# Two of four chunk inversions moved among the blocks of two projections

## The chip, the cores and the metric

One core of a Trainium2 chip runs the kernel. The metric is the device time of one execution in microseconds, as the median of several runs.

## What is computed

Two transformer blocks over 512 tokens of width 1024. The change lies in the first, whose mixer has two halves:

```python
proj = rms_norm(x, norm_w) @ w_in          # dn_q, dn_k, dn_v, dn_z, beta, decay, sw_q, sw_k, sw_v, sw_z
q, k, v = split(silu(conv5(dn_q, dn_k, dn_v)))   # depthwise over time
q = l2_norm(q) * 128 ** -0.5; k = l2_norm(k)     # 4 heads of 128
# gated delta rule, forwards and backwards (2 directions), by chunks
t_inv = inverse(I + strict_tril(beta * k k^T * decay))
a_intra = tril(q k^T * decay)
state, o = scan over the chunks with t_inv, a_intra, k, v
dn = rms_norm(fwd + bwd) * silu(dn_z)
# banded attention: window 128, 8 query heads, 2 key heads of 64, with sinks
sw = softmax_with_sink(rope(rms(sw_q)) @ rope(rms(sw_k))^T, band) @ sw_v * silu(sw_z)
x = x + concat(dn, sw) @ w_out
```

The kernel takes chunks of 128 tokens, so there are four (cb 0 to 3), each in two directions d.

## The kernel before

All engines walk one list, `ORDER`, that Python code builds by calling `do(name, ...)`. Each engine has its own function for a step's name and emits its part, so the order of the list is the order of every engine's queue: TensorE, ACT, DVE and POOL (GpSimd) are in-order, and SP issues the loads. Semaphores (`Mark`) carry the dependences. PSUM has eight banks of 128x512; `Ring.take` hands them out in turn, and the first writer of a bank waits until its last reader is done (`emptied`).

Matmuls of the projections are in three parts: every weight unit is loaded to RAW, rounded to WH by ACT (`prep`), and WL = RAW - WH is made by POOL; there are four slots. `w_ahead(u)` puts the preparation of unit u in the list, two units ahead of its use. Products of activations are taken as hi*hi + hi*lo + lo*hi.

Stages around the change, in order of the list:

- Units 8 to 19, `ch`: twelve groups of 128 channels of dn_q, dn_k, dn_v. `conv` of group j-1 stands behind `ch` of group j: ACT copies the bank with the centre tap, DVE adds four taps (line 1332), ACT applies silu, `square` (ACT) follows for groups 0 to 7. Between them stand `gates` (two steps, softplus, sigmoid and cumulated decays) and `swa_prep` (13 steps: four `rope_sq`, one root, then a scale and a turn for each of four token blocks: DVE on SWR, R1, R2).
- `tok` of SZ (units 20 to 23) and Z (24 to 27): four weight units by four token blocks in banks 0 to 3. I call the 6 matmuls of one unit and one token block a block. Each group of 16 ends with ACT's silu of the four banks into MIX.
- `qk_norm` beside SZ: `qsum` (TensorE sums squares over channels, ACT takes the logarithm), then `qexp` (ACT Exp, then the product into QK on POOL for even j and DVE for odd j). `to_tok` turns v and k to tokens, `rope_t` the attention's q and k; ACT copies each bank out. They stand in `g1`, beside Z.
- `invert(cb)`: 19 steps. Two `inv_decay` (TensorE broadcasts the decays, ACT Abs and Exp give EE, POOL makes MB with two operations), `inv_kq` (k k^T and q k^T), `inv_m` (DVE MP, POOL adds the identity, DVE masks DD, ACT rounds MR), `inv_mt` (turned MP), six doubling levels, each `inv_x` (8 matmuls, two DVE masks) and `inv_d` (16 matmuls, three ACT copies and one of DVE), `inv_x7`, `inv_t`. The work buffers of chunks 1 and 2 lie in the weight slots WH and WL, so they wait for the last block of Z.
- `swa`: 32 pieces (4 query blocks by 8 heads) as `swa_s` (scores in bank 5, maximum on DVE, Exp on ACT), `swa_t`, `swa_o`; a block of 8 heads is closed by DVE, and POOL multiplies it into MIX. 96 steps.
- Before, the four inversions take turns, one step each with two of `swa` behind it. Then `z_gain` (four POOL products) and the scan (`scan_keys`, `scan_v`, `scan_o`), which starts with POOL's `vb`.

Of the kernel before, what the change touches and what calls it, by code (L numbers as in the profile page):

```python
# [199 lines left out]
def program(nc, x, wflat, cfd, ppd, prd, wsd, tbd, seld, out):  # L200
# [9 lines left out]
    C0 = 48  # L210
# [45 lines left out]
    KT = zb("kt", [128, 4, 512], F32, 72)  # L256
    VT = zb("vt", [128, 4, 512], F32, 80)
    SL8 = [zb(f"sl{j}", [128, 512], F32, 72 + 2 * j) for j in range(8)]
# [5 lines left out]
    SKT = zb("skt", [128, 512], F32, 127)  # L264
# [21 lines left out]
    MP = [zb(f"mp{c}", [128, 2, 512], F32, 4 * c) for c in range(4)]  # L286
    AT = [zb(f"at{c}", [128, 2, 512], F32, 16 + 4 * c) for c in range(4)]

    def work(i, *at):
# [9 lines left out]
            work(3, two_at(zb, 104), two_at(zb, 108), two_at(sb, C0 + 16.25), (zb, (112, 124)))]  # L299
# [4 lines left out]
    OT = zb("ot", [128, 512], F32, 129)  # L304
# [242 lines left out]
    for j in range(12):  # L547
        w_ahead(U_CH + j + 2)
        G.take(("ch", U_CH + j), (conv_v, (j, 4)))
        do("ch", U_CH + j, "n0", 1)  # L550
        if j:
            do("conv", j - 1)
            if 2 <= j <= 9:
                do("square", j - 2)
        if j in (1, 3):
            step(g2)
        if j:
            step(g3, 2 if j > 6 else 1)
# [4 lines left out]
    G.over((0, 1, 2, 3))  # L563
    g1 = in_turn(qk_norm(), to_tokens("v"), rope_turn(), to_tokens("k"))

    def tok_part(u0, n, by, *sides):
        ids, i = G.ids, G.i
        G.over((0, 1, 2, 3))
        for tb in range(4):
            G.take(("tok", u0, tb), by(tb))  # L570
        G.ids, G.i = ids, i
        for k in range(4):
            w_ahead(u0 + k + 2)
            do("tok", u0, k, "n0", SLOT0, n)
            for g, m in sides:
                step(g, m)

    G.over((4, 5, 6, 7))
    tok_part(U_SZ, 512, lambda tb: (proj, ("sz", tb)), (g1, 3))
    gi = [invert(cb) for cb in (0, 3, 1, 2)]  # L580
    BI.over((4,))
    ids, i = G.ids, G.i
    G.over((0, 1, 2, 3))
    for tb in range(4):
        G.take(("tok", U_Z, tb), (proj, ("z", tb)))
    G.ids, G.i = ids, i
    for k in range(4):
        w_ahead(U_Z + k + 2)
        do("tok", U_Z, k, "n0", SLOT0, 512)
        step(g1, 4)  # L590
        if k in (1, 2):
            step(gi[0])
    while step(g1):
        pass
    step(gi[1], 2)
    BI.over((0, 1, 2, 3, 4))
    gs = swa()
    for b in (5, 6, 7):
        BANK[("swa", b)] = (b, emptied[b])
    for g in gi[2:]:  # L600
        step(g, 2)
    live = True
    while live:
        live = False
        for g in gi:
            live = step(g) or live
            step(gs, 2)
# [328 lines left out]
    def pool_engine(e):  # L936
# [25 lines left out]
        def inv_decay(cb, d):  # L962
            W = WORK[cb]
            ee, mb = W["EE"][d][:], W["MB"][d][:]
            on.wait_ge(*inv_a.at(("ee", cb, d)))
# [30 lines left out]
        def scan_keys(d, r):  # L996
            cb = chunk(d, r)
            W = SCAN[d]
            if r == 0:
                on.wait_ge(*inv_v.at(("t", 0, 1)))  # L1000
                on.wait_ge(*inv_v.at(("t", 2, 1)))
                on.wait_ge(*swa_g.at(3))
            else:
                on.wait_ge(*scan_p.at(("av", d, r - 1)))
            on.wait_ge(*gate_v.at("beg"))
            on.wait_ge(*gate_a.at("egl"))
            on.wait_ge(*tok_a.at(("k", cb)))
            on.wait_ge(*tok_a.at(("v", cb)))
            k3 = h3(KT[:, cb, :])
            if r:  # L1010
                e.tensor_tensor(h3(W["KB_"][:]), k3, b4r(BEG[:, d, cb, :]), ALU.mult).then_inc(scan_g.up(("kb", d, r)), 1)
            e.tensor_tensor(h3(W["VB"][:]), h3(VT[:, cb, :]), b4r(BETA[:, d, cb, :]), ALU.mult).then_inc(scan_g.up(("vb", d, r)), 1)
            if r < 3:
                e.tensor_tensor(h3(W["KD"][:]), k3, b4r(EGL[:, d, cb, :]), ALU.mult).then_inc(scan_g.up(("kd", d, r)), 1)
# [25 lines left out]
    def scalar_engine(e):  # L1040
# [67 lines left out]
        def to_tok(what, cb):  # L1108
            b, _ = BANK[(what, cb)]
            on.wait_ge(*tok_p.at((what, cb)))  # L1110
            on.wait_ge(*qk_g.at(6))
            on.wait_ge(*qk_v.at(7))
            act((VT if what == "v" else KT)[:, cb, :], psum[b][:, :], ACT.Copy, tok_a.up((what, cb)))
# [32 lines left out]
        def tok(u0, i, which, ks, n):  # L1146
            if i < 3 or u0 in (U_OUT, U_OUT2):
                return
# [15 lines left out]
        def inv_decay(cb, d):  # L1164
# [3 lines left out]
            on.wait_ge(*gate_v.at("ngc"))  # L1168
            if cb in (1, 2):
# [22 lines left out]
        def swa_s(n):  # L1192
# [3 lines left out]
            if n > 1:  # L1196
                on.wait_ge(*swa_p.at(("t", n - 2)))
            act(PM[n % 2][:, 0:nk], psum[5][:, 0:nk], ACT.Exp, swa_a.up(("p", n)), bias=MX[:, qb, h:h + 1], scale=0.125,
# [104 lines left out]
        def finish(tb):  # L1303
            for n in range(2):
# [10 lines left out]
                    gate1=gate1, gate2=gate2, rope_root=rope_root, rope_t=rope_t, tok=tok, inv_decay=inv_decay, inv_m=inv_m,  # L1315
# [6 lines left out]
    def vector_engine(e):  # L1322
# [849 lines left out]
```

## Time and profile before

| | us |
|---|---|
| median of 3 runs | 1100.96 |
| lowest and highest | 1096.2, 1101.19 |
| the profiled execution | 1095.42 |
| its span, first to last instruction | 1093.6 |
| TensorE busy | 1014.5 (93%) |
| DVE, ACT, POOL busy | 459.4, 448.7, 414.0 |
| mean granted clock of TensorE | 0.976 |

The rows below are of the profiled execution. Its span starts with the first instruction; 1.8 us lie around it. PE is TensorE's matmuls, PEld its weight loads; PEclk is the granted clock as a share of 2.4 GHz. A row of the timeline has the start, the busy time, the engine, the line of the kernel, the operation, its output and inputs, their shapes and how many instructions are merged; in brackets the idle time ahead of it and who ended it. Matmul rows overlap each other by pipelining. Lines 1044, 1326, 1329, 1332 and 1722 belong to helpers that emit ACT activations, DVE operations and matmuls, so rows are told apart by tile names.

### The profile page before, as it was taken

To read this page: it belongs to the slowest core of one execution; us is meant where nothing else is said; L and a number is where in the kernel's file an instruction comes from. 1 tells how busy PE (TensorE), PEld (TensorE's weight loads), DVE (VectorE), ACT (ScalarE), POOL (GpSimd) and SP (SyncE) were. 2 spreads that over 40 slices of the span, in tenths; PEclk is the share of its full clock that TensorE was granted. 3 is DMA by queue.
4 is the path that set the end of the run, shared out by engine and by line. 5 is a ranking of instruction groups with operands and counts; after the bars stand their busy time and mean duration, and the time that the engine had idled before them with its cause. 6 is when DMAs were issued, how large, how long until landed. Compare 5 with 4: busy or idle time off the path is not lost.

```text
span 1093.6 us, 12916 instructions
## 1 busy us (share of the span) xinstructions
PE 1014.5 (93%) x5326; PEld 839.0 (77%) x5326; DVE 459.4 (42%) x744; ACT 448.7 (41%) x800; POOL 414.0 (38%) x221
## 2 busy tenths in 40 slices
PE   5999779759999899979999999989999999999997
PEld 4887557647889898868777767878888888888876
DVE  5046922077666536240112263243333333474434
ACT  5356337724445226244234443244343434342223
POOL 2565325543002144353432323244443435354440
PEclk9999989869999999999999999989999999999999
DMA  7422212000000005332221101123323232322212
GB/s 258 149 61 83 69 58 78 1 0 1 1 1 1 1 1 183 119 115 76 78 77 59 58 1 58 58 96 99 115 79 114 81 112 83 110 96 96 96 38 77
DMA packets 22730, 80.41 MB, mean 74 GB/s; under 512 B 2480, under 2 KB 2736, under 8 KB 22544
## 3 DMA queue, kind: packets, MB, share of 16 engines
q1 hardware_dynamic: 21808, 77.95, 21.9%
q10 hardware_dynamic: 864, 1.64, 0.4%
q8 instruction: 42, 0.69, 0.3%
q14 instruction: 16, 0.13, 0.0%
HBM read 77.48 MB, written 2.10 MB: 73 GB/s over the span
## 4 chain that ended last, share of the span: by engine, by line
PE 78%; DVE 12%; ACT 7%; POOL 1%; issue 1%; DMA 1%; DVEq 0%; ACTq 0%
PE bank L1722 75%; PE bank L1730 3%; DVE qk L1332 2%; DVE swr L1326 1%; ACT L1044 1%; DVE vc L1332 1%; DVE xl L1326 1%; DVE dd L1326 1%; DVE xs L1332 1%; ACT ee L1044 1%; ACT qk L1044 1%; ACT xs L1044 1%; ACT wh L1044 1%; DVE mp L1326 1%; DVE r L1326 1%
## 5 line engine op out<-in xcount | busy, mean ns | idle before, releaser
L942 POOL TENSOR_TENSOR wl<-raw,wh 128x1024 fp32r<-128x1024 f32 (+1 forms) x131 | 315.3, 2412 | 472.2 <-ACT wh L1044 472.1
L1722 PE MATMUL bank<-xh,wh 128*128 128x512 f32 (+1 forms) x536 | 207.2, 387 | 8.7 <-DVE xl L1326 4.8
L1722 PE MATMUL bank<-xl,wh 128*128 128x512 f32 (+1 forms) x536 | 206.4, 385 | 0.0
L1722 PE MATMUL bank<-xh,wl 128*128 128x512 f32 (+1 forms) x536 | 206.3, 385 | 0.0
L1044 ACT ACTIVATE wh<-raw 128x1024 fp32r<-128x1024 f32 (+1 forms) x131 | 135.4, 1043 | 140.1 <-PE bank L1722 140.0
L1722 PE MATMUL bank<-wh,xh 128*128 128x512 f32 (+1 forms) x352 | 139.5, 396 | 16.6 <-DVE xl L1326 7.2
L1722 PE MATMUL bank<-wh,xl 128*128 128x512 f32 (+1 forms) x352 | 135.8, 386 | 0.0
L1722 PE MATMUL bank<-wl,xh 128*128 128x512 f32 (+1 forms) x352 | 135.7, 385 | 0.0
L1722 PEld LDWEIGHTS bank<-xh,wh 128*128 128x128 f32 x536 | 102.0, 190 | 30.3 <-issue 7.5
L1722 PEld LDWEIGHTS bank<-xh,wl 128*128 128x128 f32 x536 | 102.0, 190 | 19.7
L1722 PEld LDWEIGHTS bank<-xl,wh 128*128 128x128 f32 x536 | 102.0, 190 | 19.4
L1722 PEld LDWEIGHTS bank<-wh,xh 128*128 128x128 f32 x352 | 67.8, 193 | 32.2 <-issue 11.7
L1722 PEld LDWEIGHTS bank<-wh,xl 128*128 128x128 f32 x352 | 67.5, 192 | 13.1
L1722 PEld LDWEIGHTS bank<-wl,xh 128*128 128x128 f32 x352 | 67.5, 192 | 12.8 <-issue 0.9
L1326 DVE TENSOR_TENSOR al<-ac,ah 128x512 fp32r<-128x512 f32 x22 | 53.6, 2447 | 51.8 <-ACT ah L1044 51.8
L1722 PE MATMUL bank<-wh,ah 128*128 128x512 f32 x176 | 68.5, 389 | 2.9 <-DVE al L1326 2.9
L1722 PE MATMUL bank<-wl,ah 128*128 128x512 f32 x176 | 68.5, 389 | 0.0
L1722 PE MATMUL bank<-wh,al 128*128 128x512 f32 x176 | 68.5, 389 | 0.0
L1332 DVE SCALAR_TENSOR_TENSOR ta<-bank,pparams,ta 128x510 f32<-128x510 f32 (+1 forms) x44 | 32.9, 749 | 72.5 <-ACT ta L1044 71.8
L1332 DVE SCALAR_TENSOR_TENSOR tgg<-bank,pparams,tgg 128x510 f32<-128x510 f32 (+1 forms) x44 | 33.0, 749 | 62.4 <-ACT tgg L1044 61.6
L1044 ACT ACTIVATE tgg<-bank,pparams 128x512 f32<-128x512 f32 x22 | 17.2, 781 | 78.8 <-PE bank L1722 78.8
L1628 DVE TENSOR_REDUCE mx<-bank 128x1 f32<-128x128 f32 (+3 forms) x32 | 15.7, 491 | 74.9 <-PE bank L1722 74.9
(224 smaller groups left out, 1507.6 us busy)
## 6 DMA issues: line engine op xcount, KB each, us to landing
raw<-in_wflat SPq DMA_DIRECT2D x127, 512.0 KB, 3.5
h<-in_x SPq DMA_DIRECT2D x4, 512.0 KB, 5.4
h<-in_x SPq DMA_DIRECT2D x1, 2048.0 KB, 8.7
gain<-in_pr SPq DMA_DIRECT2D x3, 512.0 KB, 3.7
consts<-in_cf SPq DMA_DIRECT2D x1, 1472.0 KB, 7.0
raw<-in_wflat SPq DMA_DIRECT2D x4, 272.0 KB, 3.3
out<-outt ACTq DMA_DIRECT2D x4, 256.0 KB, 2.1
out<-outt SPq DMA_DIRECT2D x4, 256.0 KB, 2.1
```

The costliest lines, as they stand in the source:

```text
L942: e.tensor_tensor(WL[u % NS][:, 0:n], RAW[u % NS][:, 0:n], WH[u % NS][:, 0:n].bitcast(F32), ALU.subtract).then_inc(w_lo.up(u), 1)
L1044: return e.activation(out_, in_, f, **k).then_inc(up, 1)
L1326: return e.tensor_tensor(out_, a, b, op).then_inc(up, 1)
L1332: return e.scalar_tensor_tensor(out_, a, s, b, op0, op1).then_inc(up, 1)
L1628: e.tensor_reduce(mx, psum[FA_BANKS[n % 2]][:, 0:(qb + 1) * 128], AX.X, ALU.max, negate=True).then_inc(fa_v.up(("m0", n)), 1)
L1722: return e.matmul(o, l, r_, start=start, stop=stop, skip_group_check=part)
L1730: return e.transpose(o, in_, cf("ident")[0:in_.shape[0], 0:in_.shape[0]])
```

## The change

The chunks are taken in another place. `swa_prep` gives one step for each channel group from the first on, and the two `gates` steps move from groups 1 and 3 to groups 6 and 8. SZ and Z are emitted block by block: six blocks carry `qk_norm` (and two mask steps of chunk 3), the other 26 carry chunks 0 and 3, alternately one and two steps per block. Banks 4 to 7 serve `qsum` and these inversions. After the last block come the masks of chunks 1 and 2, the turning of v, rope and k (13 copies), and then chunks 1 and 2 take turns with three `swa` steps behind each.

The buffers of the stage are laid out anew: the squares SL8 lie where chunk 0's work buffers are (ACT's masks of chunk 0 wait for the last use of SL8), K and V by tokens lie in XH and XL (their copies wait for the last block of Z), chunk 3's work lies on R1, R2 and on attention's PM and PMT (POOL's mask waits for the last turn, the first two Exp of attention for chunk 3's end), and MP and AT of chunks 0 and 3 lie where KT and VT were.

```diff
-    KT = zb("kt", [128, 4, 512], F32, 72)
-    VT = zb("vt", [128, 4, 512], F32, 80)
-    SL8 = [zb(f"sl{j}", [128, 512], F32, 72 + 2 * j) for j in range(8)]
+    KT = [zb(f"kt{c}", [128, 512], F32, (12, 14, 16, 18)[c]) for c in range(4)]
+    VT = [zb(f"vt{c}", [128, 512], F32, (28, 30, 0, 2)[c]) for c in range(4)]
+    SL8 = [zb(f"sl{j}", [128, 512], F32, 32 + 2 * j) for j in range(8)]
...
-    MP = [zb(f"mp{c}", [128, 2, 512], F32, 4 * c) for c in range(4)]
-    AT = [zb(f"at{c}", [128, 2, 512], F32, 16 + 4 * c) for c in range(4)]
+    MP = [zb(f"mp{c}", [128, 2, 512], F32, (72, 4, 8, 76)[c]) for c in range(4)]
+    AT = [zb(f"at{c}", [128, 2, 512], F32, (80, 20, 24, 84)[c]) for c in range(4)]
...
-            work(3, two_at(zb, 104), two_at(zb, 108), two_at(sb, C0 + 16.25), (zb, (112, 124)))]
+            work(3, two_at(zb, 116), two_at(zb, 120), two_at(sb, C0 + 16.25), two_at(zb, 124))]
...
-        if j in (1, 3):
+        step(g3)
+        if j in (6, 8):
             step(g2)
-        if j:
-            step(g3, 2 if j > 6 else 1)
     do("conv", 11)
     for g in (g2, g3):
         while step(g):
             pass
-    G.over((0, 1, 2, 3))
-    g1 = in_turn(qk_norm(), to_tokens("v"), rope_turn(), to_tokens("k"))
...
-    G.over((4, 5, 6, 7))
-    tok_part(U_SZ, 512, lambda tb: (proj, ("sz", tb)), (g1, 3))
-    gi = [invert(cb) for cb in (0, 3, 1, 2)]
-    BI.over((4,))
...
-        do("tok", U_Z, k, "n0", SLOT0, 512)
-        step(g1, 4)
-        if k in (1, 2):
-            step(gi[0])
+    G.over((4, 5, 6, 7))
+    BI.over((4, 5, 6, 7))
+    gi = [invert(cb) for cb in (0, 3, 1, 2)]
+    g1 = qk_norm()
+
+    def both(*gs):
+        live = True
+        while live:
+            live = False
+            for g in gs:
+                if step(g):
+                    live = True
+                    yield
+
+    def tok_parts(u0, name):
...
+        for k in range(4):
+            w_ahead(u0 + k + 2)
+            for tb in range(4):
+                do("tok_b", u0, k, "n0", SLOT0, 512, tb)
+                yield
+        do("evac", u0)
+
+    dense_parts = in_turn(tok_parts(U_SZ, "sz"), tok_parts(U_Z, "z"))
+    for n in range(6):
+        step(dense_parts)
+        step(g1, 2)
+        if n in (2, 4):
+            step(gi[1])
     while step(g1):
         pass
-    step(gi[1], 2)
+    g03 = both(gi[0], gi[1])
+    n = 0
+    while step(dense_parts):
+        n += 1
+        step(g03, 2 if n % 2 else 1)
+    gs = swa()
+    g1 = in_turn(to_tokens("v"), rope_turn(), to_tokens("k"))
     BI.over((0, 1, 2, 3, 4))
-    gs = swa()
+    G.over((0, 1, 2, 3, 4))
+    step(gi[2], 2)
+    step(g1, 2)
+    step(gi[3], 2)
+    step(g1, 2)
...
+    while step(g1):
+        pass
...
-    for g in gi[2:]:
-        step(g, 2)
     live = True
     while live:
         live = False
-        for g in gi:
+        for g in gi[2:]:
             live = step(g) or live
-            step(gs, 2)
+            step(gs, 3)
     do("z_gain")
...
             on.wait_ge(*tok_p.at((what, cb)))
-            on.wait_ge(*qk_g.at(6))
-            on.wait_ge(*qk_v.at(7))
-            act((VT if what == "v" else KT)[:, cb, :], psum[b][:, :], ACT.Copy, tok_a.up((what, cb)))
+            on.wait_ge(*dense.at((U_Z + 3, 3)))
+            act((VT if what == "v" else KT)[cb][:], psum[b][:, :], ACT.Copy, tok_a.up((what, cb)))
...
             on.wait_ge(*gate_v.at("ngc"))
+            if cb == 0:
+                on.wait_ge(*qk_g.at(6))
+                on.wait_ge(*qk_v.at(7))
             if cb in (1, 2):
                 on.wait_ge(*dense.at((U_Z + 3, 3)))
...
             if n > 1:
                 on.wait_ge(*swa_p.at(("t", n - 2)))
+            else:
+                on.wait_ge(*inv_v.at(("t", 3, 1)))
...
             on.wait_ge(*inv_p.at(("q", cb)))
-            on.wait_ge(*dense.at((U_Z + 3, 3)))
+            if cb in (1, 2):
+                on.wait_ge(*dense.at((U_Z + 3, 3)))
```

## Rows read from the trace of the kernel before

**Rows 1.** The page: shares of the chain of waits by engine.

```profile
PE 78%; DVE 12%; ACT 7%; POOL 1%; issue 1%; DMA 1%; DVEq 0%; ACTq 0%
```

**Rows 2.** Busy time by stretch: stretch, length, PE, PEld, DVE, ACT, POOL, clock, DMA.

```profile
145.65:200.75 55.10, 54.24 (x241) 41.49 (x242) 5.95 (x5) 36.16 (x57) 25.46 (x14) 0.95 0.18 58
200.75:250.60 49.85, 30.27 (x179) 24.18 (x177) 28.27 (x48) 22.29 (x59) 29.45 (x25) 0.76 0.00 0
250.60:372.97 122.37, 121.62 (x972) 107.58 (x973) 79.60 (x160) 57.98 (x139) 15.00 (x12) 1.00 0.00 1
```

**Rows 3.** Timeline of DVE beside the channel groups.

```profile
62.68 3.10 DVE L1332 SCALAR_TENSOR_TENSOR qk<-bank,pparams,qk 128x510 f32<-128x510 f32 x4 [36.09 <-ACT qk L1044]
...
72.75 3.10 DVE L1332 SCALAR_TENSOR_TENSOR qk<-bank,pparams,qk 128x510 f32<-128x510 f32 x4 [0.24 <-ACT qk L1044]
...
78.60 3.10 DVE L1332 SCALAR_TENSOR_TENSOR qk<-bank,pparams,qk 128x510 f32<-128x510 f32 x4 [1.91 <-ACT qk L1044]
...
102.58 0.81 DVE L1326 TENSOR_TENSOR swr<-swr,ssq 128x640 f32<-128x640 f32 x1
...
110.89 3.02 DVE L1326 TENSOR_TENSOR swr<-swr,ssq 128x640 f32<-128x640 f32 x1
...
119.31 2.96 DVE L1326 TENSOR_TENSOR swr<-swr,ssq 128x640 f32<-128x640 f32 x1
...
135.21 3.05 DVE L1326 TENSOR_TENSOR swr<-r,r 128x128 f32<-128x128 f32 x2
```

**Rows 4.** Timeline of TensorE: three column sums (two instructions each), twice.

```profile
145.71 5.38 PE L1722 MATMUL bank<-sl,consts 128*128 128x512 f32 x6 [1.45 <-DVE vc L1332]
...
156.40 2.74 PE L1722 MATMUL bank<-sl,consts 128*128 128x512 f32 x6
```

**Rows 5.** Timeline of ACT: tables, logarithms, Exp, and one mask.

```profile
147.28 1.28 ACT L1044 ACT_TABLE_LOAD   x1
148.58 0.69 ACT L1044 ACTIVATE sl<-bank,ceps 128x512 f32<-128x512 f32 x1
...
176.58 2.18 ACT L1044 ACTIVATE sl<-sl 128x512 f32<-128x512 f32 x4
...
187.96 1.17 ACT L1044 ACTIVATE ee<-bank,ngc 128x128 f32<-128x128 f32 x4
189.16 0.63 ACT L1044 ACTIVATE ee<-ee 128x512 f32<-128x512 f32 x1
```

**Rows 6.** Timeline of POOL: weight subtraction, products of Q and K, mask.

```profile
152.84 2.40 POOL L942 TENSOR_TENSOR wl<-raw,wh 128x1024 fp32r<-128x1024 f32 x1 [3.15 <-ACT wh L1044]
...
176.14 4.69 POOL L947 TENSOR_TENSOR qk<-qk,sl 128x512 f32<-128x512 f32 x3 [2.90 <-ACT sl L1044]
...
189.87 1.28 POOL L966 TENSOR_TENSOR mb<-ee,consts 128x512 f32<-128x512 f32 x1 [2.92 <-ACT ee L1044]
191.23 1.04 POOL L968 TENSOR_TENSOR mb<-mb,nbeta 128x512 f32<-128x512 f32 x1
```

**Rows 7.** Timeline of DVE and POOL: the preparation of one chunk.

```profile
231.97 1.28 DVE L1326 TENSOR_TENSOR mp<-bank,mb 128x512 f32<-128x512 f32 x2
234.03 2.34 DVE L1326 TENSOR_TENSOR dd<-mp,consts 128x512 fp32r<-128x512 f32 x2 [0.78 <-POOL mp L980]
...
232.73 2.49 POOL L980 TENSOR_TENSOR mp<-mp,consts 128x512 f32<-128x512 f32 x2 [2.41 <-DVE mp L1326]
```

**Rows 8.** TensorE: four blocks (chain of waits); two scores, four x steps (timeline).

```profile
180.10 5.46 PE bank L1722 x24
...
336.50 0.70 PE L1722 MATMUL bank<-skt,sqt 64*128 64x256 f32 x2
...
339.72 0.70 PE L1722 MATMUL bank<-skt,sqt 64*128 64x256 f32 x2
...
351.17 3.74 PE L1722 MATMUL bank<-dt,mr 128*128 128x128 f32 x32
```

**Rows 9.** Timeline of POOL: the four gains and the scan's first product.

```profile
346.96 5.02 POOL L987 TENSOR_TENSOR mix<-mix,rparams 128x512 f32<-128x512 f32 x4
378.59 1.04 POOL L1012 TENSOR_TENSOR vb<-vt,beta 128x512 f32<-128x512 f32 x1 [26.61 <-DVE mp L1326]
```

More of the change, by code:

```diff
@@ L263, in program @@
     R2 = zb("r2", [128, 640], F32, 124.5)
-    SKT = zb("skt", [128, 512], F32, 127)
+    SKT = zb("skt", [128, 512], F32, 128)
     SQT = zb("sqt", [128, 4, 512], F32, 64)
@@ L303, in program @@
     SWO = zb("swo", [128, 512], F32, 122)
-    OT = zb("ot", [128, 512], F32, 129)
+    OT = zb("ot", [128, 512], F32, 116)
     SCAN = [dict(VB=zb("vb0", [128, 512], F32, 32), KB_=zb("kb0", [128, 512], F32, 34), KD=zb("kd0", [128, 512], F32, 36),
@@ L562, in program @@
             pass
-    G.over((0, 1, 2, 3))
-    g1 = in_turn(qk_norm(), to_tokens("v"), rope_turn(), to_tokens("k"))
-    def tok_part(u0, n, by, *sides):
+    G.over((4, 5, 6, 7))
[11 more added lines that the diff above has]
+    def tok_parts(u0, name):
         ids, i = G.ids, G.i
@@ L569, in tok_part @@
         for tb in range(4):
-            G.take(("tok", u0, tb), by(tb))
+            G.take(("tok", u0, tb), (proj, (name, tb)))
         G.ids, G.i = ids, i
@@ L573, in tok_part @@
             w_ahead(u0 + k + 2)
-            do("tok", u0, k, "n0", SLOT0, n)
-            for g, m in sides:
-                step(g, m)
-    G.over((4, 5, 6, 7))
-    tok_part(U_SZ, 512, lambda tb: (proj, ("sz", tb)), (g1, 3))
-    gi = [invert(cb) for cb in (0, 3, 1, 2)]
-    BI.over((4,))
[L582 to L588, printed above, removed]
-        do("tok", U_Z, k, "n0", SLOT0, 512)
-        step(g1, 4)
-        if k in (1, 2):
-            step(gi[0])
+            for tb in range(4):
[8 more added lines that the diff above has]
+            step(gi[1])
     while step(g1):
         pass
-    step(gi[1], 2)
-    BI.over((0, 1, 2, 3, 4))
-    gs = swa()
+    g03 = both(gi[0], gi[1])
[5 more added lines that the diff above has]
+    g1 = in_turn(to_tokens("v"), rope_turn(), to_tokens("k"))
+    BI.over((0, 1, 2, 3, 4))
+    G.over((0, 1, 2, 3, 4))
[3 more added lines that the diff above has]
+    step(g1, 2)
+    while step(g03):
+        step(g1)
+    while step(g1):
+        pass
     for b in (5, 6, 7):
         BANK[("swa", b)] = (b, emptied[b])
-    for g in gi[2:]:
-        step(g, 2)
     live = True
@@ L964, in inv_decay @@
             ee, mb = W["EE"][d][:], W["MB"][d][:]
+            if cb == 3:
+                on.wait_ge(*rope_v.at(("qo", 3)))
             on.wait_ge(*inv_a.at(("ee", cb, d)))
@@ L1008, in scan_keys @@
             on.wait_ge(*tok_a.at(("v", cb)))
-            k3 = h3(KT[:, cb, :])
+            k3 = h3(KT[cb][:])
             if r:
                 e.tensor_tensor(h3(W["KB_"][:]), k3, b4r(BEG[:, d, cb, :]), ALU.mult).then_inc(scan_g.up(("kb", d, r)), 1)
-            e.tensor_tensor(h3(W["VB"][:]), h3(VT[:, cb, :]), b4r(BETA[:, d, cb, :]), ALU.mult).then_inc(scan_g.up(("vb", d, r)), 1)
+            e.tensor_tensor(h3(W["VB"][:]), h3(VT[cb][:]), b4r(BETA[:, d, cb, :]), ALU.mult).then_inc(scan_g.up(("vb", d, r)), 1)
             if r < 3:
@@ L1146, in tok, with evac @@
         def tok(u0, i, which, ks, n):
-            if i < 3 or u0 in (U_OUT, U_OUT2):
-                return
+            if i == 3 and u0 not in (U_OUT, U_OUT2):
+                evac(u0)
+        def evac(u0):
             for tb in range(4):
@@ L1314, in scalar_engine @@
         return dict(begin=begin, prep=prep, stat=stat, split=split, conv=conv, square=square, qsum=qsum, qexp=qexp, to_tok=to_tok,
-                    gate1=gate1, gate2=gate2, rope_root=rope_root, rope_t=rope_t, tok=tok, inv_decay=inv_decay, inv_m=inv_m,
+                    gate1=gate1, gate2=gate2, rope_root=rope_root, rope_t=rope_t, tok=tok, evac=evac, inv_decay=inv_decay, inv_m=inv_m,
                     inv_d=inv_d, swa_s=swa_s, swa_t=swa_t, swa_o=swa_o, scan_keys=scan_keys, scan_v=scan_vn, scan_o=scan_o,
```

## The prediction

> **What bounds the kernel now.** I read the line that sums the chain of waits first [rows 1]: TensorE carries 78% of it, so an idle or half-clocked TensorE is what can be won or lost, and its work is the same before and after. Next the busy time by stretch [rows 2], cut where the stage changes: last convolution to the last block of the Z group (145.65 to 200.75), from there to the first doubling level (200.75 to 250.60), and on to the last of them (372.97). TensorE is busy 54.24 of 55.10 us, then 30.27 of 49.85 at a granted clock of 0.76, then 121.62 of 122.37. The loss is in the middle stretch, where the four chunks are prepared (masks, products, turning) one after another on ACT, DVE and POOL. The convolutions ahead of it are bound by ACT and DVE: TensorE waits 1.45 us for the last one and comes back at half clock, 1.2 of 2.4 GHz: three column sums take 5.38 us there and 2.74 later [rows 4].
>
> Prices of TensorE's work at the full clock [rows 4, 8]: a block (6 matmuls of 512 columns) 5.46/4 = 1.37; a column sum 2.74/3 = 0.9; a small matmul or transpose 3.74/32 = 0.115, so four transposes 0.45, x of a level (8) 0.93, d (16) 1.8, kq of a chunk (16) 1.9; a piece of attention over two key blocks 339.72 - 336.50 - 2 x 0.93 = 1.36.
>
> **Work against time before.** First stretch: 28 blocks 38.3, 8 column sums 7.2, 12 groups of transposes 5.4, two gate turns 0.8, together 51.7 of 55.1: lost 3.4. Second: one group of transposes and six gate turns 2.9, four kq 7.6, four turns of M 3.6, 7.5 pieces of attention 10.2, together 24.3 of 49.85: lost 26. Third: nothing [rows 2]. I now do the same for the new order, queue by queue.
>
> **1. Convolutions.** One channel group is a serial chain: ACT copy, four DVE operations of 0.78, ACT silu, square, weight copy: 5.85 us from one group's first DVE operation to the next, and 8.4 late in the stage, as the scales' starts show [rows 3]. The difference is the rotary work, two steps per group: 2.5 us of turning, then a scale that takes 3 us beside POOL's weight subtraction and 0.81 alone [rows 3]. One step per group fits into the 2.8 us in which DVE waits for ACT anyway. The moved gate steps cost ACT's chain 4.9 and 3.5 (5.85 to 10.75 and 9.35; gate 1 cost 10.07 for group 1, without a square, and gate 2 now waits behind 2.5 us of turning on DVE), the root 1.6, and the turn beside the subtraction for group 9 2.5. Counted from the first convolution at 62.68 [rows 3], with groups 1 to 11 at 5.4, 5.85, 5.85, 7.5, 5.85, 10.75, 5.9, 9.35, 5.85, 7.8, 4.4, the last starts at 137.2 and ends at 140.3 instead of 145.65: -5.3. But the first column sum now comes after one block of SZ, not four, and its bank (4) is freed by the last convolution. TensorE stands idle for some 11 us before it, and three blocks (4.1 us) are left for later. Net -1.2 (between -4 and +1).
>
> **2. From there to the normalised Q and K.** Now kq of chunk 3 waits in TensorE's queue for all of Q and K after only seven blocks; before, 28 blocks lay ahead. The chain is ACT's and POOL's, all from [rows 5, 6]: silu and weight copy 1.6, table load 1.3, logarithms 0 and 1 held to 4.3; 2 to 5 follow TensorE, at half clock at first, to 12.1; Abs of the first mask 1.2, table 1.3, Exp 0.6, table 1.3, two logarithms 1.2, weight copy 1.0, table 1.3, four Exp 2.4, mask 1.8, four Exp 2.1: 26.1. POOL, behind two weight subtractions, two masks and three products, ends the last product at about 29.5. TensorE has 6 blocks, 8 sums and 3 gate turns for it, 16.6: lost 12.9, against 3.4 before. +9.5. Even if all starts at full clock and POOL follows ACT at once, 26.5 us stay: +6.5; with DVE and POOL in each other's way it is +11.
>
> **3. Chunks 3 and 0 prepared among blocks.** ACT's masks of chunk 0 wait for the same product (their buffer is now the square's), so behind 29.5 come Abs, Exp, POOL's two mask operations (2.3 per direction), a weight subtraction of 2.4, and only then POOL's identity for chunk 3 (2.5), then DVE's 2.34 for two masks [rows 5 to 7]. TensorE runs kq, three blocks, kq and waits for the turning of M of chunk 3 from about 39.7 to 42.9; then its first level waits for DVE until 47.3, chunk 0's turning and levels until 53.6. To 56.4 it has done 17.8 of work in 26.9: lost 9 (3 if half clock and POOL's queue cost nothing, 14 if each block is waited for). After that a chunk's next step has the other chunk's step and 1.37 us of block ahead of it, more than one DVE mask (0.6) or an ACT copy (0.6) takes, so levels cost nothing. The group's drain (silu, table load) at block 16 delays block 17: +1.5. With 1.5 steps per block, 39 steps are on offer for the 36 that two chunks need: both end inside.
>
> **4. Chunks 1 and 2.** Their masks wait for the last block, and now the 13 copies that lay beside the Z group stand in the same ACT queue: drain 0.6, four masks at 1.8 and a table load 8.5, nine of the 13 copies ahead of the loop, 0.5 each as an Exp of the same size, 4.5: the attention's first piece can't start before 13.5 [rows 5]. In the loop: two kq 4.5 each with their first pieces, two preparations at 5.3 (DVE's 1.28 + POOL 1.3 twice + DVE's 2.34, less overlap, and a score's maximum [rows 7]), the turning 4.5: 37.5 (31 to 41). Work in it: 4 gate turns 1.6, 13 transposes 5.7, kq 3.8, M 1.8, six pieces 8.1: 21. Lost 16.5 against 26: -9.5.
>
> **5. Beside attention.** A piece per step instead of two thirds. After an x the next score has 0.93 + 1.84 before it, about what its own loop needs. I take +1 for the four places where DVE closes a block of heads, now with two chunks to cover instead of four.
>
> **6. The end.** Attention's last product now falls behind the last-but-one step, and with it POOL's queue: closing product 1.28, then the four gains of 5.02 us, and only then the scan's first product. Before, these ran at 346 to 352 under the inversions and POOL waited 26.61 us for DVE [rows 9]. After: last x end, 2.3 to DVE's result, 1.3, 5.0 = 8.6; before 372.8 to 378.59 = 5.8. +2.8, and it can't be hidden since nothing else is ready. The other side (+2, +4) is near.
>
> **Sum.** -1.2 + 9.5 + 9 + 1.5 - 9.5 + 1 + 2.8 = +13.1. The buffers' new places cost nothing themselves: no transfer is added, and the squares' old place is the late masks'. The waits that they bring are in 2 and 3. Everything behind the scan moves as a whole. Against the profiled execution, 1095.4, this gives 1108.5. That is at the foot of the runs (1096.2, 1100.96, 1101.19); for a median I take 1100: **1113**.
>
> **Rivals.**
> (a) The blocks cover the preparation fully, faster. One mechanism: POOL's order in 3 costs nothing and two chunks prepare in half the time of four (25 of 49.85) plus 5. Then 3 is 0 and 4 is a stretch of 30, lost 9, -17; with the rest +13 - 9 - 7.5 - 1 = -4.5, and with 2 at its floor -7.5: 1094. It decides as soon as 3 and 4 together lose less than 13 us, where I have 25.5. For it: DVE and ACT are under 60% busy in the middle stretch. Against: it is a chain, not a load.
> (b) All between: 1100, within 0.5%.
> (c) The score's own loop binds beside two chunks: score 0.97, maximum 0.75, exponential 0.6, up to 1.25 of DVE's masks ahead of it, 3.5 against 2.8 after each of 12 x steps: +8, 1121. For it: one bank for all scores. Against: before, score to score was 3.2 to 3.8 with TensorE full.
> (d) Both preparations go slowly, at half clock throughout: 3 at 14, 4 at 41, 2 at +11: +23, 1123.
> (e) Switching ACT's tables costs more where switches are many. The row of a load and of the first operation behind it are 1.30 us apart [rows 5], and four switches lie in the chain of 2 where two lay. Were each 1.4 dearer, +5.5: 1118.
> The Trainium skill, "ScalarE: Activation LUTs", section "What ACT_TABLE_LOAD costs", gives 1.28 us and a drain of about 1.38 for each switch; by that, (e) would hold, while the rows here have the load alone.
> That the change doesn't do what it says can't be: 39 steps for 36, fixed by the order.
>
> **Numbers.** Forecast 0.42 (1105 to 1119), (c) 0.1, (d) 0.12, (e) 0.03: slower 0.67. Within 0.5% (5.5 us, about what this measurement can tell) 0.15; faster 0.18. The range leaves out the better half of (a) and what lies above (c) and (d): 1095 to 1128.
>
> **What would show it.** Last convolution ends near 140; a TensorE gap of 10 us before kq, ended by POOL or DVE "qk"; gaps ended by "mp" and "dd" behind it; the last block near 260; POOL's four gains right before the first "vb", at 390 or later. Wrong if the gap before kq is under 5 us, if the stretch from the last block to the first level of chunk 1 is under 30, or if TensorE is less than full beside attention.

## The result, and the profile after

| | before | after |
|---|---|---|
| median, us | 1100.51 (4 runs) | 1183.26 (1181.48 to 1185.08, 4 runs) |
| ratio, 95% interval | | 1.0761 (1.0728 to 1.0794) |
| span of the profiled execution | 1093.6 | 1179.7 |
| mean granted clock | 0.976 | 0.903 |

The change makes the kernel 83 us slower. I had forecast 13 us, and the range ended at 1128.

The page of after, second part: the span in 40 slices of 29.5 us, busy tenths of TensorE and its granted clock, and then the line that sums the chain.

```profile
PE   5999567987999997999899999998999999999997
...
PEclk9999778997555557999999999998999999999999
...
PE 66%; issue 14%; DVE 8%; ACT 7%; POOL 3%; DMA 1%; DVEq 0%; POOLq 0%; ACTq 0%
```

The clock is at 0.5 in slices 11 to 15, and TensorE is busy nine tenths or more in each of them. Where before the chain had 78% of TensorE [rows 1], it has 66 now and 14% "issue": it followed POOL back through a wait of 35 us and saw no stall that would explain the time. So the windows have to be read, as in [rows 2]: stretch, length, busy us of PE, PEld, DVE, ACT, POOL, granted clock.

```profile
200.00:259.40 59.40, 59.06 (x419) 54.25 (x418) 24.44 (x37) 25.34 (x43) 4.76 (x2) 1.00 0.06 19
259.40:280.00 20.60, 14.34 (x93) 11.75 (x92) 2.19 (x5) 15.65 (x37) 9.14 (x8) 0.87 0.01 1
280.00:303.20 23.20, 16.93 (x78) 13.22 (x77) 16.32 (x29) 6.08 (x17) 10.80 (x8) 0.65 0.00 0
303.20:323.20 20.00, 20.00 (x81) 16.55 (x81) 8.26 (x18) 6.47 (x17) 1.27 (x1) 0.50 0.00 1
323.20:343.20 20.00, 20.00 (x80) 15.51 (x79) 6.88 (x14) 4.60 (x12) 0.00 (x0) 0.50 0.00 0
...
420.00:440.00 20.00, 20.00 (x84) 16.93 (x84) 7.37 (x16) 6.14 (x16) 0.65 (x1) 0.50 0.00 1
440.00:460.00 20.00, 16.44 (x103) 14.43 (x102) 8.58 (x18) 3.44 (x10) 4.34 (x4) 0.76 0.00 0
```

From 303.20, where the first doubling level of chunk 1 begins, TensorE is never idle, and yet starts only 79 to 84 instructions in 20 us, where before had 156 to 160 in the levels (260 to 320). It does so at 0.50, 1.2 GHz, up to the seventh x of the last chunk near 448; its granted clock in the same work before was full [rows 2]. The waits that the prediction walked through are there too (start, busy time, and in brackets the idle time ahead and who ended it):

```profile
137.27 3.78 PE L1745 MATMUL bank<-sl,consts 128*128 128x512 f32 x4 [11.53 <-DVE vc L1354]
...
166.14 3.75 PE L1745 MATMUL bank<-qk 128*128 128x128 f32 x16 [9.96 <-POOL qk L961]
180.68 0.66 PE L1753 MATMUL bank<-consts,mp 128*128 128x128 f32 x4 [3.34 <-POOL mp L996]
182.00 0.76 PE L1753 MATMUL bank<-consts,mp 128*128 128x128 f32 x4 [0.66 <-POOL mp L996]
187.73 1.11 PE L1745 MATMUL bank<-dt,mr 128*128 128x128 f32 x8 [2.41 <-DVE mp L1348]
...
303.20 1.95 PE L1745 MATMUL bank<-dt,mr 128*128 128x128 f32 x8
```

The last row is the first level: eight matmuls take 1.95 us, where an x has 0.93 from [rows 8] in the prediction. And the end, POOL's queue, which answers to [rows 9]:

```profile
455.66 1.28 POOL L1010 TENSOR_TENSOR mix<-mix,swo 128x512 f32<-128x512 f32 x1 [35.00 <-DVE swo L1348]
456.90 4.92 POOL L1003 TENSOR_TENSOR mix<-mix,rparams 128x512 f32<-128x512 f32 x4
461.78 1.03 POOL L1028 TENSOR_TENSOR vb<-vt,beta 128x512 f32<-128x512 f32 x1
```

The scan's first product starts at 461.78, 83.2 us later than in [rows 9]. The whole span is 86.1 us longer, so all but 2.9 us of the loss arises ahead of the scan.

### The profile page after: what moved, and what is told of

Its sections match the earlier page's. It is cut to its first block, busy times and chain, and to the rows that moved or that the text cites. A ratio compares the mean times of both kernels' runs of the same rounds, so it can differ in the third digit from the quotient of the medians.

```text
span 1179.7 us, 12917 instructions
## 1 busy us (share of the span) xinstructions
PE 1088.0 (92%) x5326; PEld 899.1 (76%) x5326; DVE 462.4 (39%) x744; ACT 452.9 (38%) x800; POOL 414.9 (35%) x221
## 4 chain that ended last, share of the span: by engine, by line
PE 66%; issue 14%; DVE 8%; ACT 7%; POOL 3%; DMA 1%; DVEq 0%; POOLq 0%; ACTq 0%
PE bank L1745 64%; PE bank L1753 2%; DVE qk L1354 2%; ACT L1060 1%; DVE vc L1354 1%; ACT ee L1060 1%; DVE xl L1348 1%; ACT wh L1060 1%; DVE xs L1354 1%; ACT qk L1060 1%; ACT xs L1060 1%; ACT sl L1060 1%; POOL at L990 0%; DVE dd L1348 0%; POOL kb L1027 0%
## 5 line engine op out<-in xcount | busy, mean ns | idle before, releaser
L1745 PEld LDWEIGHTS bank<-wh,xh 128*128 128x128 f32 x352 | 67.6, 192 | 22.3 <-issue 9.0
L1010 POOL TENSOR_TENSOR mix<-mix,swo 128x512 f32<-128x512 f32 x4 | 5.1, 1272 | 152.1 <-DVE swo L1348 152.1
L1060 ACT ACTIVATE pm<-bank,mx 128x256 f32<-128x256 f32 (+1 forms) x32 | 16.9, 527 | 97.1 <-DVE mx L1351 97.1
```

The costliest lines, as they stand in the source:

```text
L1010: e.tensor_tensor(MIX[:, qb, 512:1024], MIX[:, qb, 512:1024], SWO[:], ALU.mult).then_inc(swa_g.up(qb), 1)
L1060: return e.activation(out_, in_, f, **k).then_inc(up, 1)
L1745: return e.matmul(o, l, r_, start=start, stop=stop, skip_group_check=part)
```

## The experiments

Theory A, formed on these rows: the levels with attention beside them keep whichever clock TensorE has when they begin; before came to them at full, after at half. Theory B: three attention steps per round, instead of two, are a mix that holds the clock down. All comparisons of a ratio are against runs of the kernel before on the same chip.

**Fewer attention steps, in after and more of them in before.**

```diff
 # after
-            step(gs, 3)
+            step(gs, 2)
 # before
-            step(gs, 2)
+            step(gs, 3)
```

> The changed kernel with two attention steps behind each inversion step of chunks 1 and 2 instead of three; what is left of attention follows behind the inversions. The changed kernel ran from 300 to 448 us at a granted clock of 0.50 with TensorE busy throughout. Theory A (entry): the clock fell in the gaps of the preparation just before, and the steps that follow, of whatever mix, don't bring it back; then this run stays at half clock from 300 on and takes 1170 to 1190. Theory B (mix): a whole piece of attention beside each step holds the clock down; then two thirds of a piece, as in the kernel before, let it rise and the time is 1105 to 1120.

Measured: 1123.64 us (one execution), a little above what theory B gave and far below theory A's. This looked like theory B, until the windows were read: the clock was 0.50 from 290 to 301, came up between 301 and 302, when the first level had just begun (301.66), and stayed at 1.00 up to 360. So the entry itself was different here, and the run doesn't decide between the theories.

> The kernel before with three attention steps behind each inversion step instead of two. Theory A (entry): its preparation has about the gaps of before, the clock comes back near 250, and the time is 1095 to 1110. Theory B (mix): the clock stays at 0.50 as long as attention lasts, some 32 steps and 32 pieces, about 75 us of work: 1150 to 1180.

Measured: 1100.77 us (one execution), 3.2 above the median of before on the same chip. The clock rose between 258 and 259, ahead of the first level at 263.97. Three steps per round, TensorE full, granted clock 1.00:

```profile
240.00:256.00 16.00, 12.01 (x44) 7.87 (x44) 12.33 (x22) 4.17 (x11) 8.05 (x7) 0.50 0.01 2
260.00:280.00 20.00, 20.00 (x152) 16.17 (x151) 14.57 (x31) 7.11 (x20) 2.67 (x3) 1.00 0.00 1
280.00:300.00 20.00, 20.00 (x152) 16.30 (x151) 12.88 (x28) 9.75 (x26) 1.27 (x1) 1.00 0.00 1
```

Theory B falls: the same mix of three steps holds full clock.

**A burst ahead of the levels.** Six column sums of 512 columns (12 instructions, of which nothing is used) in a free bank, right before the first level:

```diff
+    rounds = 0
     while live:
         live = False
+        if rounds == 3:
+            BI.take("warm", (warm_p, "end"))
+            do("warm")
+        rounds += 1
         for g in gi[2:]:
             live = step(g) or live
...
+            for i in range(6):
+                t = mm(p[:, :], cf("ones"), QK[:, i % 8, :], True, True)
```

> The changed kernel with six extra fp32 matmuls of 512 columns (about 5 us at the full clock, results unread) between the preparation of chunks 1 and 2 and their first level. Theory A (entry): the burst raises the clock and the steps behind it keep it at 1.00: 1183 - 74 + 5, so 1108 to 1120, which would also give the cost of the change without the clock (forecast +13). Theory B (mix): the clock falls back to 0.50 within the following steps, and the time stays within 1170 to 1190.

Measured: 1121.82 us (1121.29 to 1122.51), ratio 1.022 (1.0203 to 1.0237). Timeline and windows of this kernel, TensorE:

```profile
304.13 7.12 PE L1751 MATMUL bank<-qk,consts 128*128 128x512 f32 x12
```

```profile
304.00:307.00 3.00, 3.00 (x6) 1.45 (x6) 0.00 (x0) 0.74 (x3) 0.00 (x0) 0.50 0.00 0
308.00:312.00 4.00, 4.00 (x16) 2.19 (x14) 0.32 (x1) 0.00 (x0) 0.00 (x0) 1.00 0.00 0
312.00:332.00 20.00, 20.00 (x147) 15.95 (x147) 13.64 (x30) 9.49 (x25) 1.26 (x1) 1.00 0.01 2
```

The first 3 us of the burst pass at 0.50; the clock rises between 307 and 308, and from there to the end of the levels it is at 1.00. The mix of work is that of after, three steps per round, and 7.1 us of added work take 61 us off the median (1183.26 to 1121.82, on two chips; the ratios to before are 1.076 and 1.022). In 20 us TensorE now starts 147 instructions, not 81. The clock is the cause of that part: the levels keep the clock at which they are entered.

**Attention taken away from beside the levels** (it runs behind them):

```diff
         for g in gi[2:]:
             live = step(g) or live
-            step(gs, 3)
```

> The changed kernel with no attention beside the inversions of chunks 1 and 2; all of it follows behind them, one piece after another. Theory A (entry): the levels start after a stretch with gaps and are bound by their own latency with two chunks, clock 0.50 there too. Theory B (mix): the levels alone reach 1.00. In both, attention alone then waits for its own loop of score, maximum, Exp (about 2.5 us a piece, 80 us): 1150 to 1230. The clock of the two stretches is what tells, not the time.

Measured: 1189.49 us (one execution). The levels alone don't raise the clock either:

```profile
290.00:300.00 10.00, 10.00 (x49) 10.00 (x48) 5.25 (x9) 2.98 (x5) 7.45 (x7) 0.50 0.01 2
310.00:330.00 20.00, 20.00 (x95) 20.00 (x95) 7.88 (x12) 7.16 (x12) 0.00 (x0) 0.50 0.00 0
330.00:350.00 20.00, 20.00 (x96) 20.00 (x96) 8.30 (x12) 6.89 (x12) 0.00 (x0) 0.50 0.00 1
```

The clock rose just after 354, in the x7 steps that follow the levels and without any added work: there pairs of 128-column matmuls alternate with bf16 transposes. In after it rose in the same steps, between 448 and 449.

**A small burst in the middle of the levels.** Sixteen matmuls of 128 columns in full precision (32 instructions) at the ninth round, and in a sister kernel six column sums of 512 columns at the same place:

```diff
+        if rounds == 8:
+            BI.take("warm", (warm_p, "end"))
+            do("warm")
+        rounds += 1
...
+                t = mm(hs(p, i % 4), cf("ones"), QK[:, i % 8, 0:128], True, True)
```

> The same place as the burst midway, but 16 matmuls of 128 columns in full precision in place of the six column sums of 512. If it is the width of a matmul that brings the clock back, it stays at 0.50 behind them and the time is that of the kernel after plus 2 to 4 us, 1185 to 1188 us. If any run of full-precision matmuls brings it back (the last levels of the kernel before's copy without attention beside came up in x7, which is small work), 1.00 behind them and about 1150 us. If the clock is up by itself before the levels, about 1120 us, and nothing is told.

Measured: 1146.56 us. The burst, and the clock around it:

```profile
362.92 5.10 PE L1751 MATMUL bank<-qk,consts 128*128 128x128 f32 x32
367.77 1.09 PE L1751 MATMUL bank<-xf,dd 128*128 128x128 f32 x8
```

```profile
364.00:365.00 1.00, 1.00 (x7) 1.00 (x6) 0.00 (x0) 0.00 (x0) 0.00 (x0) 0.50 0.00 0
365.00:366.00 1.00, 1.00 (x8) 1.00 (x8) 0.00 (x0) 0.00 (x0) 0.00 (x0) 0.67 0.00 0
366.00:367.00 1.00, 1.00 (x12) 1.00 (x11) 0.00 (x0) 0.00 (x0) 0.00 (x0) 1.00 0.00 0
```

The clock rises in the burst, after 59 us of levels at 0.50, and stays at 1.00 behind it (from 384 to 404 TensorE starts 158 instructions at 1.00). So theory A holds both ways within one execution, and the width of a matmul alone isn't what keeps the clock down: a plain run of 128-column matmuls does it, where the levels' 128-column matmuls, as busy by the profile, don't.

> The kernel after, with six column sums of 512 columns (12 instructions that nothing uses) put among TensorE's work in the middle of the levels of chunks 1 and 2, at the ninth round of the loop, instead of ahead of them. Theory A (a row of levels and attention keeps whichever clock it began with, and wide work raises it): granted clock 0.50 until the burst, with durations as in the kernel after, then 1.00 in every stretch behind it; with about half of the 145 us of half-clocked work done at the full clock, about 1150 us. Rival (this mix of levels and attention falls back to half clock wherever the engine has nothing else behind it): 0.50 again within some 10 us of the burst, 1185 to 1190 us. If the kernel comes up at the full clock by itself before the levels, as the one with a burst of two did, the run says nothing on this and shows about 1122 us.

Measured: 1121.39 us. Here the clock came up at 303, ahead of the burst, although TensorE's work up to there is the same as after's. The entry isn't fixed by the order of the work.

**Is it chance?** After itself, both kernels with a burst midway, and a kernel with two column sums behind the levels, each repeated on one chip:

> The kernel after itself, unchanged, timed again in five rounds. If which clock the levels run at is chance in each execution: the times scatter between about 1182 and 1118 us. If it is fixed by the kernel: all within 1180 to 1186 us, granted clock 0.50 from the entry of the levels to their end. If it is a matter of the chip: another single value for all of them.

> The kernel with six column sums midway in the levels, unchanged, which came up by itself ahead of its burst. Chance in each execution: times at 1121 us and at about 1150 us (up at the burst only) mixed. Fixed by the kernel: all at 1121 us (1119 to 1123).

> The kernel with 16 small matmuls midway, unchanged, which came up only in its burst. Chance in each execution: times at 1147 us and 1118 us mixed. Fixed by the kernel: all at 1147 us (1145 to 1149).

> The kernel after with two column sums behind the levels, so that all of TensorE's work up to their end is the same as after's, in a program whose code is two sums longer. Fixed by the order of the work: 1183 to 1185 us, 0.50 through the levels. If anything else of a build or an execution decides at which clock the levels begin: 1116 to 1120 us, or both.

| kernel | single executions, us |
|---|---|
| after again | 1181.65, 1183.58, 1184.91, 1184.94 |
| wide burst midway | 1120.26, 1150.34, 1121.81, 1121.59 |
| small burst midway | 1120.85, 1149.09, 1150.82, 1121.53 |
| two sums behind the levels | 1111.18, 1183.12, 1184.62, 1185.28 |

The executions fall on the two or three values that theory A gives and on nothing between: up before the levels (1111, 1121), up at the burst (1150), not up at all (1183 to 1185). One program takes either course. Only the first of each four was profiled; for the others the course is read from the time and the mean clock (0.967 for 1111.18, 0.900 to 0.903 for 1183 to 1185). The execution at 1111.18:

```profile
284.00:304.00 20.00, 14.41 (x64) 10.76 (x64) 14.93 (x26) 5.82 (x17) 10.79 (x8) 0.57 0.00 0
304.00:324.00 20.00, 20.00 (x148) 16.12 (x147) 13.97 (x30) 9.71 (x27) 1.26 (x1) 1.00 0.00 1
324.00:344.00 20.00, 20.00 (x151) 16.42 (x150) 12.55 (x28) 9.98 (x26) 1.27 (x1) 1.00 0.01 2
```

A us at a time, this execution first and then after, over the last preparation:

```profile
296.00:297.00 1.00, 0.00 (x0) 0.00 (x0) 0.96 (x4) 0.54 (x3) 1.00 (x2) 0.50 0.00 0
...
302.00:303.00 1.00, 1.00 (x6) 0.53 (x5) 0.32 (x2) 0.00 (x0) 0.00 (x0) 0.50 0.00 0
303.00:304.00 1.00, 1.00 (x10) 1.00 (x10) 0.43 (x2) 0.50 (x3) 0.00 (x0) 0.95 0.00 0
```

```profile
297.00:298.00 1.00, 0.60 (x2) 0.29 (x2) 0.94 (x2) 0.62 (x3) 1.00 (x2) 1.00 0.00 0
298.00:299.00 1.00, 1.00 (x9) 0.98 (x9) 0.67 (x3) 0.00 (x0) 1.00 (x2) 0.71 0.00 0
...
302.00:303.00 1.00, 1.00 (x7) 1.00 (x7) 0.64 (x2) 0.00 (x0) 0.00 (x0) 0.50 0.00 0
303.00:304.00 1.00, 1.00 (x7) 1.00 (x7) 0.00 (x0) 0.84 (x3) 0.00 (x0) 0.50 0.00 0
```

In both, TensorE is idle twice for 2 to 3.4 us in front of the turning of M and then works without a break, from 297.07 and 297.40 on. In the one the clock had been at half all through the gaps and rose just after 303, six us into the work. In after it stood at 1.00 through the last gap and fell near 298.4, when TensorE was already busy again; less than 5 us later the levels began, and it didn't rise.

The clock in the last gap isn't the whole answer, though. Five profiled executions had 0.50 in it and rose between 302 and 304, ahead of the levels (both wide bursts midway, the second small one, the burst of two below and the one above). The first small burst midway had 0.50 in its last gap too, worked without a break from 297.46, began its levels at 304.09, and did not rise:

```profile
292.00:312.00 20.00, 18.00 (x72) 13.72 (x72) 11.90 (x21) 4.07 (x12) 7.81 (x6) 0.50 0.00 1
```

The burst of six did the same up to its burst at 304.13, and so did the kernel with the gains early, below, up to its burst at 303.31: five rose and three didn't.

The Trainium skill, "TensorE: Matmul & The Clock Gate", section "Part 1: The HAM clock gate", says that the gate judges how busy TensorE has been in windows that run free of the kernel, so that the same kernel meets it differently from run to run. The table agrees in that executions of one program differ; it can't show the windows, and it leaves open why after came out alike eight times of eight. The same section says that sustained matmul activity releases the gate; the rows of after from 303 to 440 don't agree for this mix.

**The order of the convolutions alone**, in before:

```diff
-        if j in (1, 3):
+        step(g3)
+        if j in (6, 8):
             step(g2)
-        if j:
-            step(g3, 2 if j > 6 else 1)
```

> The kernel before with one part of the change alone: one rotary step per channel group from the first on, and the gate steps at groups 6 and 8. In the changed kernel the last convolution's first waiter started at 137.3 us instead of 145.7. If the order of these steps on DVE is the cause, nearly all of it shows here, less what TensorE has left of its blocks: -4 to -8 us, ratio 0.993 to 0.997. If TensorE's clock after the longer gap takes it back, within 2 us.

Measured: 1089.5 us (1087.93 to 1090.81, 6 runs), ratio 0.9921 (0.99 to 0.9941). The first column sums, at 145.71 in [rows 4]:

```profile
137.78 5.10 PE L1721 MATMUL bank<-sl,consts 128*128 128x512 f32 x6 [1.45 <-DVE vc L1331]
```

7.9 us earlier, and the kernel 8.6 us faster, with the interval of the ratio clear of 1: this part of the change is a gain, larger than my 5.3, and it is the fastest kernel of the study.

**Three repairs of after**, each on top of a burst. POOL's four gains ahead of the loop:

```diff
+    do("z_gain")
     live = True
...
-    do("z_gain")
```

> The burst kernel with POOL's four gains put ahead of the loop of chunks 1 and 2 instead of behind it. In the burst kernel POOL closes attention at 395.9 to 397.1, multiplies the gains until 402.0 and only then starts the scan's first product. If the gains in POOL's order are what delays the scan (forecast +2.8 in all, of which the gains are 5.0), 3.5 to 5 us come off against the burst kernel's 1121.8, down to 1117 to 1118.5. Rival: DVE's last products or half clock bind there anyway, under 1.5 us.

Measured: 1115.64 us (1113.42 to 1118.89), 6.2 below the burst alone. TensorE waits 2.71 us for the first `vb`, not 6.44, and starts on it 5.1 us earlier in the profiled executions (398.06 against 403.16): 3.7 us from the wait, 1.4 from ahead of the levels, where the burst began earlier and met half clock for less of its length. The four executions are two near 1113.5 and two at 1117.5 and 1118.9, so the 6.2 is a middle and not a value that was seen.

Six more blocks ahead of the inversions of chunks 0 and 3, then two steps per block:

```diff
+    step(dense_parts, 6)
     while step(dense_parts):
         n += 1
-        step(g03, 2 if n % 2 else 1)
+        step(g03, 2)
```

> The burst kernel with six more blocks ahead of the inversions of chunks 0 and 3, and then two steps for each of the 20 that are left, so that TensorE has 8.2 us of work for the wait of 10 us for Q and K. If that wait is lost time (forecast +9.5 for the stretch), 6 to 9 us come off 1121.8: 1113 to 1116. Rival: the preparation of chunks 3 and 0 moves back with them and now has fewer blocks beside it, so that the gain is given back: above 1119.

Measured: 1116.12 us (1115.54 to 1116.83), 5.7 below the burst alone. The wait for the normalised Q and K shrinks from 9.97 to 1.96. In the profiled executions the first `vb` starts 8.0 us earlier than in the burst kernel; 1.7 of these are the burst itself, which here ran at full clock (5.37 us against 7.12), since the clock had risen just ahead of it:

```profile
168.12 2.02 PE L1752 MATMUL bank<-qk 128*128 128x128 f32 x16 [1.96 <-issue]
178.68 1.11 PE L1760 MATMUL bank<-consts,mp 128*128 128x128 f32 x4 [3.52 <-POOL mp L1003]
```

Two column sums in place of six:

> The burst kernel with two column sums instead of six (3.6 us at half clock). Theory A (entry) says that what counts is whether the clock rises before the levels start: if these two are enough, the time is 1121.8 - 3 and the levels run at 1.00; if not, the levels stay at 0.50 and the time is about 1185. Anything between, with the clock rising in the middle of the levels, speaks for another cause of the rise than the burst.

Measured: 1118.06 us (1117.66 to 1119.97). In the profiled execution the clock had risen before the two sums (at 303, the sums start at 303.29), so this one doesn't show what they do. The count does: with column sums ahead of the levels, in five kernels, all 22 executions came to the levels at full clock (12 of 12 in the three whose TensorE work up to there is after's, this one among them); without them, after and the three kernels above, 7 of 22 did.

All three, with two column sums:

> The kernel after with three repairs together: two column sums of 512 columns ahead of the levels of chunks 1 and 2, POOL's four gains ahead of the loop, and six more blocks before the inversions of chunks 0 and 3 begin. If the three costs (clock, end, wait for Q and K) are separate terms: 1118.1 - 6 - 5.7 = 1106 us, ratio to before 1.007 (1104 to 1109). If the early gains and the later inversions take from the same slack (POOL busy where the loop begins): 1110 to 1116. If the clock isn't back before the levels, 1165 to 1175. In no case below the kernel before, since the waits of the preparation of chunks 0 and 3, about 9 us, are still in.

Measured: 1106.22 us (1103.09 to 1108.67, 6 runs), ratio 1.0066 (1.0043 to 1.0089). The terms give 1118.1 - 6.2 - 5.7 = 1106.2. That the median hits this to the tenth is luck: three executions lie at 1103.1 to 1103.9 and three at 1108.5 to 1108.7, none between. Within these 3 us the terms add up. What is left, 7 us above before and some 17 us above the order of the convolutions alone, I put down to the preparation in two portions; no run takes that away.

**Bursts in before.** The new order of the convolutions, and two column sums behind the preparation of each of the four chunks:

```diff
+            if rounds == 1:
+                BI.take(("warm", n), (warm_p, n))
+                do("warm", n)
```

> The kernel before with the changed order of the convolutions alone (which measured 0.992 of before), and two column sums of 512 columns that nothing uses behind the preparation of each of the four chunks, where TensorE waits in the kernel before too, and where its granted clock was 0.76 on the mean. If wide work in the waits keeps the clock up in that stretch: the half-clocked part of its 30 us of work gets up to twice as fast, -1 to -4 us against the order alone, ratio 0.989 (0.986 to 0.992). If the stretch is a chain of ACT, DVE and POOL which TensorE's clock hardly touches, as the three engines' rows say: the eight sums are hidden or cost up to 4 us, ratio 0.992 to 0.996.

Measured: 1093.62 us (1092.26 to 1096.1, 9 runs), ratio 0.9962 (0.9947 to 0.9976), 4 us above the order alone. The mean clock from 193 to 240 rises from 0.75 to 0.82 and nothing is won; the first level comes 2.9 us later (248.14 against 245.29). As in the expectation's second case, the clock hardly touches a stretch bound by the chain of ACT, DVE and POOL, and the sums cost time of their own. In this kernel work added for the clock's sake paid only ahead of the stretch which TensorE bounds.

## Why the prediction was wrong, step by step

The step that failed is 5, "beside attention", priced at +1, together with the clock it took over from the third stretch of [rows 2]. It asked whether attention's own chain keeps up with a piece per step, which it does, and took TensorE's prices at full clock because the levels had run at full before. The levels cost 159.8 us from the first x (303.20) to the scan's first product (462.96) where the execution at full clock needs 92.2 (303.41 to 395.59): 67.6 of the 83.2 us (after, then the execution at 1111.18, then the scan's start in before):

```profile
462.96 4.04 PE L1745 MATMUL bank<-vb,mp 128*128 128x128 f32 x16 [6.44 <-POOL vb L1028]
```

```profile
303.41 1.09 PE L1748 MATMUL bank<-dt,mr 128*128 128x128 f32 x8
...
395.59 3.65 PE L1748 MATMUL bank<-vb,mp 128*128 128x128 f32 x16 [4.69 <-POOL vb L1031]
```

```profile
379.78 3.69 PE L1722 MATMUL bank<-vb,mp 128*128 128x128 f32 x16 [3.25 <-POOL vb L1012]
```

Rival (d) had half clock in the preparations alone, and its +23 reached nowhere near. My test, "wrong if TensorE is less than full beside attention", looked at busy share and would have passed: TensorE was 20.00 of 20.00 busy.

The rest can be judged by the execution at 1111.18 us, in which `vb` follows 15.8 us later than before (395.59 against 379.78 on TensorE; its two column sums lie in the wait ahead of `vb`). The sum on record was +13.1. That it comes so near is partly luck: by the prediction's own measure, time less work at full-clock prices, step 1 was 3.1 too dear and steps 3 and 4 were 3.8 and 6.3 too cheap, which leaves about -2 for step 5 at full clock, where I had +1. The rows below are those of after, whose stages up to the first level start within 1 us of that execution's.

- Step 1, convolutions: first column sum at 137.27, predicted 140.3, and TensorE idle for 11.53, predicted 11. The mechanism was right and the gain undersized, 8.4 instead of 5.3, so that the net was -4.3 and not -1.2; alone it is worth 8.6 us.
- Step 2, the wait for Q and K: from the last convolution to kq of chunk 3 28.9 us, predicted 29.5; a wait of 9.96 ended by POOL "qk". The term comes to +8.9, against +9.5. (The ACT chain's items add up to 26.3, not 26.1.) Shown by removal: with six blocks more in front, 5.7 us come back.
- Step 3, chunks 3 and 0 among blocks: waits of 3.34, 0.66, 2.41 and 0.34 ended by POOL "mp", DVE "mp" and ACT "mix", 6.8 us of idle time. The 9 on record counted half-clocked work as lost too; so counted, 27.9 us from 166.14 to 194.00 hold 15.1 of work (6 blocks, 60 small matmuls and transposes): lost 12.8, undersized and inside its bound of 14. Levels beside blocks cost nothing, 59.06 of 59.40 us busy at full clock; the drain at block 16 cost 0.34, not 1.5. The last block ends at 259.4, predicted near 260.
- Step 4, chunks 1 and 2: the loop starts 14.2 us behind the last block, predicted 13.5, but the first level comes after 43.8 us, not 37.5 and above my upper bound of 41: lost 22.8, so the term was -3.2 and not -9.5. Most of the 6.3 us are in 280 to 303.2, where TensorE is busy 16.93 us at a clock of 0.65; I had costed its work there at full clock. That would be the same omission as in 5, on a small scale, but no run isolates it: in the same stretch DVE's mask at 292.73, beside POOL's products into `at`, took 3.43 us, the one before it 2.34.
- Step 6, the end: the wait for POOL's first `vb` is 6.44 us, 3.25 before, +3.2 against +2.8. Taking the gains away from there took 3.7 us off the wait, more than the term, since before had a wait of its own in that place; the rest of the 6.2 between the medians has other sources.
- Rivals (a) and (b) are excluded by the same rows: 3 and 4 together lost 35.6 us, where (a) needed less than 13. (c) is excluded by the execution at full clock: TensorE is 20.00 of 20.00 us busy beside two chunks. (e) too: the four table loads of step 2 are in the walk at 1.3 each and it came to 28.9 us, where (e) needed 35; the operation behind each load starts 1.3 us after the load (138.85 and 140.14 for the first).

What decides whether the clock is up at the first level stays open. Before was between 1095 and 1101 us in all of its executions. After stood at half clock in eight of eight, by their times, while three programs with the same work of TensorE up to that point came up in seven of fourteen (the wide burst midway four of five, the small one two of five, the sums behind one of four). The two profiled executions of after have the same course of the clock from 296 to 308, within 0.07 in each us. So something else than the order of the work seems to shift the odds, and no run here isolates it. Which property of the levels keeps them from raising the clock isn't settled either; that it isn't attention beside them, nor the width of 128 columns alone, was shown. Nor do runs show what the remaining 2.9 us behind the scan's start are.

## What to carry to other kernels

A stretch in which TensorE is the bound can have two prices, and here the clock at its entry chose between them: before moving a long row of small matmuls behind a stage full of waits, read the granted clock in the last microseconds ahead of it, in the kernel's own trace, and forecast both cases. A stretch with full busy digits and a low PEclk digit shows no wait; the chain of this profile had it as "issue". Count instructions per stretch. The cure is cheap: a few matmuls back to back at the entry, here 7 us for 61, and 22 executions of 22; where the chain of the other engines was the bound they were pure cost. And try the parts of a change singly: the one here that was worth having (0.992) was buried under the other.

## What the runs showed that I had not expected

- TensorE busy without a break stayed at 0.50 for 145 us (303 to 448 in after), and the levels alone, without attention, for 60 (290 to 350), while the levels with attention begun at 1.00 stayed at 1.00 for 80 us (304 to 384 in the execution at 1111.18).
- A run of 32 small instructions back to back, from 362.92, raised the clock between 365 and 366, in the middle of such a stretch.
- The clock fell while TensorE was busy again (298.4 in after, work since 297.40), so the low clock of a gap can begin behind its end. A gap passed at 0.50 didn't settle it either: five executions then rose ahead of the levels or the burst, three didn't.
- One program on one chip had executions of 1111 and of 1185 us, with mean clocks of 0.967 and 0.903.
